# ScalarE takes projection units two behind TensorE's order and merge units one behind, VectorE merge units one behind

## The reference, cut to what matters

```python
z = jnp.einsum('btd,de->bte', x, p['w_in']) + p['b_in']
u, v, yg, xb, c, q, f, i, go, gz = jnp.split(z, SPLIT_POINTS, axis=-1)
o_a, v_rows = chunk_sgu(u, v, ...)                      # norm of v, causal 128x128 mixing
h, h_new = rg_lru(causal_conv(xb, ...), h0, ...)        # conv, gates, scan
o_b = jax.nn.gelu(yg) * h
o_c, pool_new = pool_mixer(c, ...)                      # window means, product
o_d, s_new = hgrn2(q, f, i, go, s0, lb, norm_g)         # 4 heads, gated linear recurrence
proj = jnp.einsum('btgc,gcd->btgd', branches, p['w_branch'])
gates = jax.nn.sigmoid(gz.reshape(B, T, N_BRANCH, D_MODEL))
y = jnp.einsum('btd,de->bte', jnp.sum(gates * proj, axis=2), p['w_out'])
```

## Time and profile before

| | |
|---|---|
| median of three runs | 1579.42 us |
| the profiled execution | 1580.33 us |
| its span, first to last instruction | 1578.5 us |
| TensorE matmul busy | 1411.7 us (89%) |
| TensorE weight loads busy | 1170.5 us (74%) |
| VectorE busy | 730.0 us (46%) |
| ScalarE busy | 533.9 us (34%) |
| GpSimd busy | 224.3 us (14%) |
| mean granted TensorE clock | 0.953 of full |

### The profile page before, as it was taken

One profiled execution on the slowest core, in us unless ns is written; L12 is line 12 of the kernel. 1 busy time (PEld: TensorE's weight loads), 2 busy tenths in 40 slices (PEclk: granted clock), 3 DMA queues, 4 the chain that ended last, 5 costly groups with the idle time before them and its releaser, 6 DMA issues.

```text
span 1578.5 us, 18624 instructions
## 1 busy us (share of the span) xinstructions
PE 1411.7 (89%) x7329; PEld 1170.5 (74%) x7329; DVE 730.0 (46%) x1059; ACT 533.9 (34%) x727; POOL 224.3 (14%) x207
## 2 busy tenths in 40 slices
PE   4989989899896859889999999998798599999996
PEld 3767768677685748778999988777586488888872
DVE  5014234133344455774222234023244789899855
ACT  1233332413423014331110001134312377888750
POOL 4200000000004242223233300001100100010011
PEclk9999999999998979999999999999998699999998
DMA  9523304133001112222333460024743489999954
GB/s 325 194 97 102 107 28 135 42 107 101 16 1 40 47 54 61 60 61 71 93 109 112 125 226 27 27 107 155 271 167 114 157 332 411 410 413 413 413 193 155
DMA packets 151219, 239.84 MB, mean 152 GB/s; under 512 B 6176, under 2 KB 108761, under 8 KB 142817
## 3 DMA queue, kind: packets, MB, share of 16 engines
q1 hardware_dynamic: 129200, 177.98, 32.3%
q0 software_dynamic: 14832, 52.57, 9.3%
q10 hardware_dynamic: 7105, 8.15, 1.6%
HBM read 214.08 MB, written 24.60 MB: 151 GB/s over the span
## 4 chain that ended last, share of the span: by engine, by line
PE 45%; DMA 2%; DVE 2%; issue 1%; ACT 1%; POOL 0%; DVEq 0%; POOLq 0%; SPq 0%; ACTq 0%
PE bank L1059 43%; DMA kv_k<-in_cache_mem_k_dram 1%; PE bank L1491 1%; PE bank L1376 1%; ACT kv_t L729 1%; PE bank L1079 1%; DVE x_tok L2198 0%; PE bank L1499 0%; DVE small L2188 0%; DMA kv_v<-in_cache_mem_v_dram 0%; DMA yb<-expert_rows,ints 0%; DMA xg<-x_scratch,table 0%; ACT pT L729 0%; DMA expert_rows<-y_out 0%; DVE xgT_lo L2159 0%
## 5 line engine op out<-in xcount | busy, mean ns | idle before, releaser
L1059 PE MATMUL bank<-xT,ring 128*128 128x288 f32 x1152 | 296.9, 418 | 0.0
L1059 PEld LDWEIGHTS bank<-xT,ring 128*128 128x128 f32 x1152 | 223.4, 196 | 63.7 <-issue 1.7
L1972 DVE TENSOR_TENSOR expert_weights_lo<-expert_weights,expert_weights_hi 128x2048 fp32r<-128x2048 f32 x96 | 218.4, 2289 | 35.0 <-ACT expert_weights_hi L983 33.8
L983 ACT ACTIVATE expert_weights_hi<-expert_weights 128x2048 fp32r<-128x2048 f32 x96 | 182.7, 1916 | 21.7 <-PE bank L1059 15.2
L1059 PE MATMUL bank<-x_hi,gate_weights_hi 128*128 128x288 f32 x512 | 167.7, 328 | 16.8 <-DVE ob L1759 11.9
L1059 PE MATMUL bank<-x_lo,gate_weights_hi 128*128 128x288 f32 x512 | 155.2, 303 | 0.0
L1059 PE MATMUL bank<-x_hi,gate_weights_lo 128*128 128x288 f32 x512 | 154.9, 303 | 0.0
L1059 PE MATMUL bank<-ob,branch_weights 128*128 128x288 f32 (+1 forms) x512 | 134.5, 405 | 0.0
L877 ACT ACTIVATE gate<-bank,pc 128x288 f32<-128x288 f32 x64 | 31.7, 501 | 272.2 <-PE bank L1059 272.1
L1059 PEld LDWEIGHTS bank<-x_hi,gate_weights_hi 128*128 128x128 f32 x512 | 101.0, 197 | 20.8 <-DVE ob L1759 12.0
L1059 PEld LDWEIGHTS bank<-ob,branch_weights 128*128 128x128 f32 x512 | 93.4, 189 | 20.3
(11 more groups left out here) (404 smaller groups left out, 2185.1 us busy)
## 6 DMA issues: line engine op xcount, KB each, us to landing
expert_weights<-in_e_wg_dram SPq DMA_DIRECT2D x32, 1024.0 KB, 9.5
expert_weights<-in_e_wu_dram SPq DMA_DIRECT2D x32, 1024.0 KB, 10.0
expert_weights<-in_e_wd_dram SPq DMA_DIRECT2D x32, 1024.0 KB, 9.8
gate_weights<-in_w_in_dram SPq DMA_DIRECT2D x32, 512.0 KB, 4.3
ring<-in_w_in_dram SPq DMA_DIRECT2D x24, 512.0 KB, 6.7
branch_weights<-in_w_branch_dram SPq DMA_DIRECT2D x32, 256.0 KB, 3.8
kv_k<-in_cache_mem_k_dram POOLq DMA_DIRECT2D x8, 1024.0 KB, 7.7
kv_v<-in_cache_mem_v_dram POOLq DMA_DIRECT2D x8, 1024.0 KB, 5.8
```

The source lines that it names most:

```text
L983: act.activation(w_hi[n % HIS][:], w_raw[n % RAW][:], ACT.Copy).then_inc(w_hi_done, 1)
L1059: return pe.matmul(out, lhsT, rhs, start=start, stop=stop)
L1972: dve.tensor_tensor(w_lo[n % RAW][:], w_raw[n % RAW][:], w_hi[n % HIS][:].bitcast(F32), ALU.subtract).then_inc(w_lo_done, 1)
```

## The change

A new function reorders the list for one engine. `late` says by how many units of its kinds an engine lags: such a step is held, and the oldest held step is put out when more are held than its kind allows. Other steps pass the held ones. Ahead of a head's `prep` all is put out up to the units of `q`, `f` and the previous head's `go` that the head needs. ScalarE walks the list with projection and `kv` units two late and merge units one late; VectorE with merge units one late. TensorE, GpSimd and the DMA queues keep their order. No instruction's work changes. Lines of the changed kernel are 17 higher than those before.

```diff
+def taking_order(steps, late):
+
+    out, held = [], []
+    for step in steps:
+        if step[0] in late:
+            held.append(step)
+            while len(held) > late[step[0]]:
+                out.append(held.pop(0))
+            continue
+        if step[:2] == ("hgrn", "prep"):
+            needed = [("z", g, h, n) for g, h in (("q", step[2]), ("f", step[2]), ("go", step[2] - 1)) for n in range(2)]
+            while any(n in held for n in needed):
+                out.append(held.pop(0))
+        out.append(step)
+    return out + held
...
-            for step in steps[NT:]:
+            for step in taking_order(steps[NT:], {"z": 2, "kv": 2, "merge": 1}):
                 if step[0] == "z":
                     z_out(step)
...
-            for step in steps:
+            for step in taking_order(steps, {"merge": 1}):
                 if step[0] == "hgrn":
                     hgrn(step[1], step[2])
```

## The result

Four runs of the changed kernel took 1524.52 us in the median (1522.18 to 1525.38), four of the kernel before 1580.05 (1579.22 to 1581.26): a ratio of 0.9646, with a 95% interval of 0.9629 to 0.9662. The span of the profiled execution fell from 1578.5 to 1523.6 us, by 54.9. The forecast was 1522, in a range of 1508 to 1545.

A forecast was written before the change was run, and what follows sets the result against it. TensorE, busy 1411.7 of 1578.5 us, was taken as the bound, so gains come only from its idle or lower-clock time. Terms: 37.5 - 4.3 + 25 - 1 = 57.2 us gained, giving 1522 us, range 1508 to 1545.

The forecast's parts named there:

- Part 1: Stage of the four recurrent heads: 37.5 us gained (30 to 39), from TensorE's idle time and lower-clock stretches that go.
- 27.4 us of idle time: Heads' stage: TensorE's waits for turned keys (17.3 us) and inside the levels (10.1 us), all counted as gone.
- six such stretches behind waits of over 2 us: Heads' stage: lower-clock stretches of TensorE, 1.7 us lost in each, 10.1 us counted as gained.
- The eleven waits: Heads' stage: TensorE's four waits of 4.33 us for turned keys and seven inside the levels, 10.1 us, forecast to go.
- Part 2: Last head: 4.3 us lost (3 to 6), as `x_hi` starts behind `norm`; TensorE's wait grows from 11.9 to 16.2.
- Part 3: Pool stage: 25 us gained (21 to 28); waits before the `wp` products go, 4 us stay for the first conv.
- Part 4: `lru` stage: 1 us lost (9 lost to 7 gained); 20 us removed, 21 added by the held-back merge sigmoid and lower clock.
- 4, 6 and 6 us: `lru` stage: new waits of TensorE on the held-back merge sigmoid in three heads, from 6.4 us worked out for each.
- The sooner conv: `lru` stage: VectorE's conv starts up to 4 us sooner, no longer behind the newest merge unit, which shortens the wait.
- The later convs' waits: `lru` stage: TensorE's conv waits of 2.1 and 7.0 us, counted as removed.
- VectorE bounds the `lru` stage: Rival, chance 0.22: VectorE's load and GpSimd's splits lose 9 to 12 us beyond the forecast in `lru`, about 1533 us.
- PSUM runs dry: Rival for slower, chance 0.03: in the heads' levels TensorE waits for banks ScalarE evicts too late, costing 72 us, 1595.

## Why the prediction came out right, and where it did not

**Part 1 was right in its waits and undersized in its clock term.** All 27.4 us of idle time went; the changed kernel's stage is all TensorE work. The term that failed is "six such stretches behind waits of over 2 us", 10.1 us: TensorE's busy time fell by 393.47 - 377.89 = 15.6 us for the same products. By the granted clock in narrow windows, the kernel before has nine such stretches in the stage, not six. The other three, in windows of 10 us (the clock is the figure ahead of the last two), stand where TensorE was busy throughout and no wait of over 2 us lies in the 20 us ahead:

```profile
72.00:82.00 10.00, 10.00 (x38) 7.69 (x37) 0.00 (x0) 2.11 (x3) 0.00 (x0) 0.89 1.00 385
...
272.00:282.00 10.00, 10.00 (x48) 8.62 (x48) 0.00 (x0) 1.43 (x4) 0.89 (x1) 0.83 0.38 109
...
382.00:392.00 10.00, 10.00 (x36) 7.33 (x35) 0.00 (x0) 2.46 (x4) 0.00 (x0) 0.86 0.52 157
```

The first of them is there in the changed kernel, too (73.02 to 77.02 above); the other two are gone. Summed over windows of 0.5 us, the lower clock cost 15.1 us before and costs 1.7 now: 13.4 won where I had 10.1. The other 2.2 of the 15.6 are not the clock; they stand at the waits. Two groups of eight level products, with the wait of 1.01 us at 240.39 between them, took 1.05 and 1.16 us, and without it the sixteen take 1.95:

```profile
221.83 1.95 PE L1076 MATMUL bank<-tmp 128*128 128x128 f32 x16
```

The eleven waits would have to take 0.2 us each for this, an estimate of which these rows show one case. Counting stretches behind long waits misses both terms.

**Part 2** was right: 16.25 us of wait where 16.2 was forecast, and the run with `x_hi` first shows that the order on ScalarE is the cause.

**Part 3** was right in size, 24.68 for 25, and in its steps: no wait ahead of a `wp` product, and 4.89 us for the first conv where I took 4. That GpSimd's bias of `v` stretches VectorE there was seen (1.21 for 0.17 us), but moving it gained nothing.

**Part 4** had the mechanism right and its size wrong: 6.5 us lost, not 1. The term that failed is "4, 6 and 6 us" of wait. The waits are 0.15, 4.97, 9.09 and 6.92, together 21.1 where I had 16, and these 5.1 us are nearly the whole miss. I worked out 6.4 us for each head from one head's chain. The kernel before showed that the two others differ: from their products in TensorE's timeline

```profile
647.03 1.43 PE L1059 MATMUL bank<-tmp,wr 128*128 128x512 f32 x2 [2.12 <-DVE tmp L1837]
...
685.96 2.08 PE L1059 MATMUL bank<-conv_odd,wr 128*128 128x512 f32 x2 [4.83 <-DVE conv_odd L1837]
```

to the end of the first merge sigmoid behind them in ScalarE's

```profile
663.38 0.90 ACT L877 ACTIVATE gate<-bank,pc 128x288 f32<-128x288 f32 x2
...
699.66 0.89 ACT L877 ACTIVATE gate<-bank,pc 128x288 f32<-128x288 f32 x2
```

are about 16.8 us and 14.2. Less 7.5 us of TensorE's work these give 9.3 and 6.7, within 0.3 of what was measured. Part of the third head's chain is a collision with GpSimd. VectorE's timeline of the changed kernel

```profile
588.67 2.11 DVE L1879 TENSOR_TENSOR_SCAN tmp<-tmp 128x576 f32<-128x576 f32 x1
...
590.88 2.10 DVE L1881 COPY att_m<-tmp 128x8 f32<-128x8 f32 x1
```

has 2.11 and 2.10 us where 1.36 and 0.16 stand without a split beside them (617.65 and 619.12 of the kernel before), and GpSimd's has the split:

```profile
589.65 3.31 POOL L2318 TENSOR_TENSOR gate_weights_lo<-gate_weights,gate_weights_hi 128x1024 fp32r<-128x1024 f32 x1
```

In the runs with `x_hi` ahead of the norm and with units one late this split comes later, the two take 1.36 and 0.75 us, 2.1 less in all, and the third wait is 6.98 us, also 2.1 less. The sooner conv did shorten the second head's chain, to 12.2 us from 13.9, although a split took 2.9 of it there. The later convs' waits went, as counted. The lower clock came out near its size: 7 us gained and 5 lost were counted, and TensorE's busy time fell by 1.5 us (121.19 to 119.69).

**The rivals.** That VectorE bounds the `lru` stage was wrong as the main cause: with VectorE's order and work unchanged the stage fell to 123.85 us. Its mechanism, single collisions with GpSimd, is real, though. The Trainium skill (SBUF - State Buffer, "Who interferes with whom") has VectorE and GpSimd share ports under an exclusive lock; the runs agree, with 2.35 us for 0.28 beside a split of 2.66. A split does not always cost VectorE its whole length, as the prediction had it: the one of 3.31 us in the third head cost 2.7. That PSUM runs dry costs 1.2 us of waits even at three late. The parts that came out wrong, 5.5 us more in the heads and 5.5 less in `lru`, have opposite signs; that the total is nearer than its terms is luck.

## What to carry to other kernels

An engine that takes work strictly in order should take a bank's eviction late, when the chain that others wait for is the next thing in its list; one unit late brought nearly all of it here, and two cost nothing as long as banks cover them. The same lag hurts where a long chain follows: ahead of such a chain, put out what is held, at a place where the table it needs is loaded anyway (that alone was worth some 16 us here). Work out the wait of every head from its own rows, and the loss to the clock from the windows of the whole stage.

## What was not expected of the hardware

TensorE ran at the lower of its levels also inside stretches in which it was never idle. In the kernel before two such stretches, at 275 and 381 us, lost 1.7 us each, both behind the sixteen products of 128x8 near a head's end. With the waits for the keys and the levels gone or down to 0.45 us, each run here still has one or two, at the stage's start or behind such products, and not behind the same head in every run. The 32 products that follow them in the first head, in the changed kernel and, at the lower clock, with three units late:

```profile
167.03 7.15 PE L1076 MATMUL bank<-ring,memT 128*128 128x256 f32 x32
...
164.90 8.84 PE L1076 MATMUL bank<-ring,memT 128*128 128x256 f32 x32
```

Why the clock falls behind one head and not behind another was not tried. And the cost of GpSimd beside VectorE moves rather than goes: 0.17 us became 1.21 and 2.20 in one order, 0.28 became 2.35 in another.
